# Activation loads two chunks ahead, first gate loads two chunks sooner, and a new spread of single-row work in a two-layer decoder kernel

## The reference, cut to what matters

```
q      = xn @ w_q                          # 8 heads, two halves of 128
v1,i1  = top16(q1 . k1) ; v2,i2 = top16(q2 . k2)
ids, g = top16 of (v1 + v2), softmax       # 16 experts of 16384, per head and token
act    = u[ids] . x                        # 128 experts for each token
w      = g * gelu(act)
y      = sum over experts of w * v[ids]
```

## Time and profile before

| | us |
|---|---|
| median of 3 runs | 3242.73 (3241.24 to 3245.43) |
| the profiled execution, its own time | 3249.34 |
| its span, first to last instruction | 3247.5 |
| TensorE busy in the span | 3202.2 (99%) |
| DVE busy | 2597.5 (80%) |
| ACT busy | 1508.2 (46%) |
| POOL busy | 1191.4 (37%) |
| mean granted TensorE clock | 0.998 |

### The profile page before, as it was taken

The page is one execution under the profiler, slowest core; times in us unless marked ns, Lnnn a source line. Parts: engine busy times, 40 slices in busy tenths (PEclk is TensorE's granted clock), DMA queues, the critical chain, the costliest instruction groups (busy, mean ns, idle before and its releaser), DMA issues.

```text
span 3247.5 us, 54682 instructions
## 1 busy us (share of the span) xinstructions
PE 3202.2 (99%) x19694; PEld 3000.9 (92%) x19694; DVE 2597.5 (80%) x4972; ACT 1508.2 (46%) x2298; POOL 1191.4 (37%) x789
## 2 busy tenths in 40 slices
PE   8999999999999999999999999999999999999998
PEld 7878888999999999999988788889999999999998
DVE  6654449999998889999866544499999888999997
ACT  5553233477773333333345532334777633333333
POOL 1000014335435656555300000143454456665552
PEclk9999999999999999999999999999999999999999
DMA  4214422589999999999821143225999999999996
GB/s 148 78 53 143 142 90 91 194 326 386 400 398 399 357 389 390 413 409 416 310 91 66 53 156 130 97 100 189 346 391 393 405 393 370 390 398 417 415 411 258
DMA packets 232172, 893.29 MB, mean 275 GB/s; under 512 B 23856, under 2 KB 69088, under 8 KB 184128
## 3 DMA queue, kind: packets, MB, share of 16 engines
q1 hardware_dynamic: 112912, 455.25, 37.2%
q0 software_dynamic: 99024, 355.98, 27.8%
q10 hardware_dynamic: 20064, 79.91, 6.2%
HBM read 809.57 MB, written 81.48 MB: 274 GB/s over the span
## 4 chain that ended last, share of the span: by engine, by line
PE 63%; issue 14%; DMA 12%; DVE 8%; POOL 2%; ACT 1%; SPq 0%; DVEq 0%; POOLq 0%; ACTq 0%
PE bank L1506 18%; PE bank L1508 18%; PE bank L1507 18%; DMA act_in<-act_d 9%; PE bank L1815 4%; DVE h L1383 4%; DVE w_lo L1411 2%; POOL lo L568 1%; PE bank L1624 1%; PE bank L1661 1%; DMA rows<-in_u_rows,ids 1%; PE bank L1642 1%; DMA raw<-in_stream 1%; DVE lo L983 1%; ACT hi L626 1%
## 5 line engine op out<-in xcount | busy, mean ns | idle before, releaser
L626 ACT ACTIVATE hi<-raw 128x2048 fp32r<-128x2048 f32 (+2 forms) x338 | 620.6, 1836 | 692.9 <-PE bank L1508 396.1
L1506 PE MATMUL bank<-xT_hi,hi 128*128 128x344 f32 (+1 forms) x2688 | 918.7, 342 | 2.1 <-DVE xT_lo L1033 1.7
L1508 PE MATMUL bank<-xT_hi,lo 128*128 128x344 f32 (+1 forms) x2688 | 905.1, 337 | 0.0
L1507 PE MATMUL bank<-xT_lo,hi 128*128 128x344 f32 (+1 forms) x2688 | 900.3, 335 | 0.0
L983 DVE TENSOR_TENSOR lo<-raw,hi 128x2048 fp32r<-128x2048 f32 (+2 forms) x320 | 698.4, 2183 | 183.1 <-ACT hi L626 180.9
L1506 PE MATMUL bank<-w_hi,hi 128*128 128x344 f32 x2048 | 662.3, 323 | 19.2 <-DVE w_lo L1411 18.6
L1507 PE MATMUL bank<-w_lo,hi 128*128 128x344 f32 x2048 | 655.0, 320 | 0.0
L1508 PE MATMUL bank<-w_hi,lo 128*128 128x344 f32 x2048 | 654.0, 319 | 0.0
L615 POOL DMA_INDIRECT rows<-in_v_rows,ids x256 | 426.1, 1665 | 301.6 <-DVE h L1383 248.2
L1506 PEld LDWEIGHTS bank<-xT_hi,hi 128*128 128x128 f32 x2688 | 504.2, 188 | 32.3 <-issue 5.9
L1508 PEld LDWEIGHTS bank<-xT_hi,lo 128*128 128x128 f32 x2688 | 504.4, 188 | 25.3
(11 more groups left out here) (258 smaller groups left out, 4108.8 us busy)
## 6 DMA issues: line engine op xcount, KB each, us to landing
raw<-in_stream SPq DMA_DIRECT2D x352, 1024.0 KB, 7.6
gate_in<-gate_d SPq DMA_DIRECT2D x96, 384.0 KB, 12.4
act_d<-act_s ACTq DMA_DIRECT2D x92, 352.0 KB, 6.3
gate_d<-gate_s ACTq DMA_DIRECT2D x22, 1472.0 KB, 9.6
act_in<-act_d SPq DMA_DIRECT2D x92, 352.0 KB, 10.0
gate_d<-gate_s ACTq DMA_DIRECT2D x22, 576.0 KB, 13.7
gate_in<-gate_d SPq DMA_DIRECT2D x32, 256.0 KB, 9.6
rows<-in_u_rows,ids POOLq DMA_INDIRECT x256, 10.0
```

The lines of the kernel that those rows point to most:

```text
L626: act.activation(hi[s][:, 0:n], raw[s][:, 0:n], ACT.Copy).then_inc(hi_done, 1)
L1506: pe.matmul(dst, a_[0], b_[0], start=first, stop=False)
L1507: pe.matmul(dst, a_[0], b_[1], start=False, stop=False)
L1508: return pe.matmul(dst, a_[1], b_[0], start=False, stop=last)
```

## The change

It has three parts.

1. The activation of a spilled chunk c is loaded by SP in the place where that of chunk c-2 was loaded before, into one of four buffers, `act_in[0]`, `act_in[1]`, `act_k[0]`, `act_k[1]` by c modulo 4. It waits for `w_lo` of chunk c-4. The four buffers have a semaphore each. ACT's loop over the last stretch runs over four chunks instead of two.
2. The four gate parts of the first slot are issued after the weight loads of q = 48 and 49 instead of 50 and 51.
3. The row operations: 84 instead of 96 by q = 42, and then shares of 41 for an up step, 28 for a kept down step and 24 for a spilled down step. ScalarE's gelu of the rows' dot products and the weighing after it move from q = 70 and 74 to q = 66 and 70.

```diff
-ROWS_IN_G = 96
+ROWS_IN_G = 84
-SHARED = 2
+SHARED, ACT_BUFS = 2, 4
-GATES_AT = {50: (0, 0), 51: (0, 2), 52: (1, 0), 53: (1, 1), 54: (1, 2), 55: (1, 3),
+GATES_AT = {48: (0, 0), 49: (0, 2), 52: (1, 0), 53: (1, 1), 54: (1, 2), 55: (1, 3),
-GATES_FROM, V_FROM = 50, 80
-ROW_GELU_AT, WEIGH_ROWS_AT = 70, 74
-UP_SHARE, DOWN_SHARE, ROWS_END = 16, 13, 2 * C_U - 2
+GATES_FROM, V_FROM = 48, 80
+ROW_GELU_AT, WEIGH_ROWS_AT = 66, 70
+UP_SHARE, KEPT_SHARE, DOWN_SHARE, ROWS_END = 41, 28, 24, 2 * C_U - 2
...
-    shares = [UP_SHARE if x in UP_OF else DOWN_SHARE for x in range(FIND_STEPS + G_STEPS, ROWS_END)]
+    shares = [UP_SHARE if x in UP_OF else KEPT_SHARE if DOWN_OF[x] < KEPT else DOWN_SHARE for x in range(FIND_STEPS + G_STEPS, ROWS_END)]
...
-        act_ld = [sem(f"act_ld{s}") for s in range(2)]
+        act_ld = [sem(f"act_ld{b}") for b in range(ACT_BUFS)]
...
+        def spilled_acts(b):
+            return (act_in, act_k)[b // 2][:, b % 2]
+
+        def acts_loaded(l, c):
+            b = c % ACT_BUFS
+            first = KEPT + (b - KEPT) % ACT_BUFS
+            return act_ld[b], 16 * (l * len(range(first, C_V, ACT_BUFS)) + (c - first) // ACT_BUFS + 1)
...
-                def load_act(j, s):
+                def load_act(v, x):
+                    j, s, b = v * ACT_BUFS // 2 + x // 2, x % 2, x % ACT_BUFS
                     wait_alone(sp, act_out[s], 16 * (l * ACT_PAIRS + j) + 16, sp_passed)
-                    sp.wait_ge(w_done, done + 2 * j + s + 1)
-                    sp.dma_start(act_in[:, s].rearrange("p i t -> p (i t)"), act_d[2 * j + s - KEPT]).then_inc(act_ld[s], 16)
+                    sp.wait_ge(w_done, done + ACT_BUFS * v + x - ACT_BUFS + 1 + CR)
+                    sp.dma_start(spilled_acts(b).rearrange("p i t -> p (i t)"), act_d[ACT_BUFS * v + x - KEPT]).then_inc(act_ld[b], 16)
...
                         load_raw(lp + P_V + v * V_CHUNKS // 2 + c // 2, c % 2)
-                        if not (isinstance(v, int) and v * V_CHUNKS + c < KEPT):
-                            load_act(v * V_CHUNKS // 2 + c // 2, c % 2)
+                        if not last or c + 2 < V_CHUNKS:
+                            load_act(v, c + 2)
...
-                        dve.wait_ge(act_ld[s], 16 * (l * ACT_PAIRS + (c - KEPT) // 2 + 1))
+                        dve.wait_ge(*acts_loaded(l, c))
```

More of the change, by code:

```diff
@@ L472, in acts_of @@
         def acts_of(k, s):
-            return (act_k, act_s, act_in)[k % SPAN // 2][:, s] if isinstance(k, int) and k < KEPT else act_in[:, s]
+            return (act_k, act_s, act_in)[k % SPAN // 2][:, s]
+        def spilled_acts(b):
[4 more added lines that the diff above has]
+            return act_ld[b], 16 * (l * len(range(first, C_V, ACT_BUFS)) + (c - first) // ACT_BUFS + 1)
         @block.sync
@@ L936, in _, with weights_hi @@
                             store_gates(q // PER_SLICE)
-                def weights_hi(c, s):
+                def weights_hi(c, s, b):
                     act.wait_ge(prod_done, l * C_V + c + 1)
@@ L943, in weights_hi @@
                         act.wait_ge(w_used, 2 * (lp + P_V) + c + 1)
-                    act.activation(w_hi[:, s], acts_of(c, s), ACT.Copy).then_inc(w_hi_done, 1)
+                    acts = acts_of(c, s) if isinstance(c, int) and c < KEPT else spilled_acts(b)
+                    act.activation(w_hi[:, s], acts, ACT.Copy).then_inc(w_hi_done, 1)
                 for q in range(FIND_STEPS + G_STEPS, C_V + KEPT):
@@ L952, in _ @@
                     if q + 1 in DOWN_OF:
-                        weights_hi(DOWN_OF[q + 1], (q + 1) % 2)
+                        weights_hi(DOWN_OF[q + 1], (q + 1) % 2, DOWN_OF[q + 1] % ACT_BUFS)
                     if q in UP_OF:
@@ L958, in _, with v_steps @@
                             store_act(UP_OF[q] // 2, q % 2)
[L960 to L968, removed]
+                def v_steps(v, first, end):
+                    for x in range(first, end):
+                        ahead(lp + P_V + v * ACT_BUFS // 2 + x // 2, x % 2)
+                        weights_hi(v * ACT_BUFS + x + 1, (x + 1) % 2, (x + 1) % ACT_BUFS)
+                v_steps(KEPT // ACT_BUFS, KEPT % ACT_BUFS, ACT_BUFS)
+                with act.Fori(KEPT // ACT_BUFS + 1, C_V // ACT_BUFS - 1) as v:
+                    v_steps(v, 0, ACT_BUFS)
+                v_steps(C_V // ACT_BUFS - 1, 0, ACT_BUFS - 1)
                 if l + 1 < DEPTH:
@@ L1400, in weigh_step @@
                     else:
-                        dve.wait_ge(act_ld[s], 16 * (l * ACT_PAIRS + (c - KEPT) // 2 + 1))
+                        dve.wait_ge(*acts_loaded(l, c))
                     dve.wait_ge(gate_ld[v % 2], 16 * GATE_PARTS * (v // 2 + 1))
-                    a_ = acts_of(c, s).rearrange("p i (q t) -> p i q t", t=SLICE)
+                    acts = acts_of(c, s) if c < KEPT else spilled_acts(c % ACT_BUFS)
+                    a_ = acts.rearrange("p i (q t) -> p i q t", t=SLICE)
                     i = 2 * (c % V_CHUNKS)
@@ L1410, in weigh_lo @@
                     dve.wait_ge(w_hi_done, k + 1)
-                    dve.tensor_tensor(w_lo[:, s], acts_of(c, s), w_hi[:, s].bitcast(F32), ALU.subtract).then_inc(w_done, 1)
+                    acts = acts_of(c, s) if c < KEPT else spilled_acts(c % ACT_BUFS)
+                    dve.tensor_tensor(w_lo[:, s], acts, w_hi[:, s].bitcast(F32), ALU.subtract).then_inc(w_done, 1)
                 assert rows_by(ROW_GELU_AT - 1) >= U_ROW_OPS and rows_by(WEIGH_ROWS_AT - 1) <= U_ROW_OPS + E
```

## The result

The changed kernel takes 3276.5 us (3275.2 to 3284.2, 4 runs) against 3244.1 us before (4 runs): ratio 1.0102, 95% interval 1.008 to 1.0124. It is 1% slower: by 32 us between the medians, and by 28.4 us between the spans of the two profiled executions. The forecast was 3238 within 3223 to 3255.

What follows compares the result with a forecast made beforehand. TensorE was taken as busy 3202 of 3247.5 us, so only waits, about 36 us, could be won. The terms -17.4 + 0 + 5 + 8.2 = -4.2 us gave a forecast of 3238, range 3223 to 3255.

Steps and rivals of the forecast that it cites:

- The last stretch: From q 82 on: earlier activation loads and fewer bytes leave 4 us of waits in both layers, -17.4 us.
- The signs named for it: In the profile after: no DVE wait for `act_in` loads in the last stretch, which takes 346 to 349 us.
- Rival E: Last stretch: sooner activation loads only put weight loads later, half of 21 us stays; +2.5 us, 3245; chance 0.10.
- q 43 to 57: Nine more rows and sooner gate parts; 121 us a layer taken, no change; upper end +6.6 us.
- q 58 to 69: Six more rows, all in up steps: 2.5 us a layer, +5 us; ends 0 and +18.
- q 70 to 81: More rows of `v` make DVE too long, 4.1 us a layer: +8.2 us; ends 0 and +13.4.
- A wait in pieces need not cost the clock's 2.7 us: q 43 to 57: short separate waits might avoid the 1.2 GHz loss seen in q 52 to 57, softening the byte limit.
- a credit of 4.4 us for seven row buffers: q 43 to 57 and q 70 to 81: half of the drained buffers, 1.8 MB, counted against the DMA time.
- Rivals C: Up steps slower by DMA bytes, 7.98 us a step against 7.57: +7.6 us, 3250; chance 0.18.
- D: q 58 to 64 slower by POOL, from about 2.0 us for each gather: +9 us, 3251; chance 0.10.
- The gates: q 43 to 57: four gate parts two steps sooner move the same late load two steps forward, to chunk 50.
- DVE's length in q 70 to 77: Four or five `v` rows a step delay DVE: waits of 2.7 us and 1.4 us, together 4.1 us a layer.

Runs made afterwards that it cites:

- part 3 alone: The kernel before with only the new row shares, 84 rows by q = 42, gelu and weighing at q = 66 and 70: ratio 1.0102.
- part 2 alone: The kernel before with only the first four gate parts issued two chunks sooner: ratio 0.9997 (0.9987 to 1.0006).

## Why the prediction was wrong

**The last stretch: right in size, and in its reason.** Forecast -17.4 us, measured -19.5. The reckoning in bytes (3.20 MB a step too much, 3.08 just enough) is borne out from three sides: part 1 gives 3.7 us in one trace and 1.6 in another, near the scatter, part 3 alone 17 (11.3 and 5.6), and half the gather bytes all of it. The signs named for it came too: no wait for `act_in`, and 345.9 and 346.8 us for the stretch (346 to 349 forecast). Rival E's mechanism, loads that come sooner only make others late, is what part 1 does by itself.

**The steps that failed** are the three terms for q 43 to 81, all of them too small and over their upper ends:

| term | taken | upper end | measured |
|---|---|---|---|
| q 43 to 57 | 0 | +6.6 | +14.4 |
| q 58 to 69 | +5 | +18 | +19.6 |
| q 70 to 81 | +8.2 | +13.4 | +15.0 |

(In the second, 1.3 us are the faster up steps of the trace before, which leaves 18.3, at the upper end.)

**First, the clock.** "A wait in pieces need not cost the clock's 2.7 us" was false here. Pieces of 1.8 and 1.9 us cost it as well, 1.6 us each, though three of 1.4 to 1.6 us did not. Slow steps cost 18 us in the changed kernel and 4.2 before; of the difference 2.3, 6.5 and 5.2 us lie in the three terms. These 14 us of the 32.6 between forecast and profile stood in no term; they are over two fifths of the error. Without them the last term would be 9.8, near its 8.2, and the middle one, without the 1.3 as well, 11.8; the first would still be 12.1 where nothing was expected. The prediction had the row (0.94 in q 52 to 57) and counted it as a loss to be won back, but didn't ask whether each new wait would bring one.

**Second, bytes set against the time of too many steps, and buffers as credit.** The bytes of q 43 to 57 were set against all 15 steps, 124.3 us at most. But 38 of the 55 rows are asked for in the first nine: these moved 79.8 x 0.409 = 32.6 MB, 79.2 us at 412 GB/s against the 68.1 that TensorE needs, while the six down steps behind them had room (375 GB/s) and took about as long as before. The nine steps alone took 6.6 and 7.2 us more. Against the bytes stood a credit of 4.4 us for seven row buffers that could be drained; it made 3.3 us a layer into nothing here, and in q 70 to 81 it brought the bytes from 6.7 to 2.3 us, under DVE's 4.1. DVE waited 11.7 us for rows in q 43 to 51 of the first layer alone. How much the buffers really gave wasn't measured by itself.

**Third, two limits at one place.** Rivals C (bytes) and D (POOL) were priced one at a time, each on top of a forecast that took the other as light. The runs show both at work in the up steps: with either one lifted, q 46 to 51 stays 6.5 to 10.6 us over its least, and with both lifted it is at it. Even the upper ends of C and D together, -17.4 + 6.6 + 18 + 13.4 = +20.6, lie 8 us under what was measured. D's condition, about 2.0 us for each gather, was met with gathers halved (1.99) and not in the changed kernel itself (46.0 / 26 = 1.77 in q 58 to 63), where its counterweight is at work: gathers fall to 0.96 us when DVE waits, but by then TensorE is waiting as well.
The Trainium skill (SBUF — State Buffer, "SBUF: two separate sides") gives the lock between DVE and GpSimd, for some kinds of DVE instruction, as one that is held for the whole instruction. The 1.9 to 2.0 us against 0.96 agree with a gather that has to wait out a row operation of DVE; which port it waits at, and whether these row operations are of the kinds named, no run here shows.

**The gates** did what was said: the late load moved two steps forward (TensorE waits for chunk 50 with part 2 alone, for chunk 52 before). In the changed kernel that is mixed with late rows.

**DVE's length in q 70 to 77** was worked out as 4.1 us a layer, and that was about right: with gathers halved, where DVE waits for no row, q 70 to 81 takes 4.7 and 5.1 us over its least, 3.1 and 5.1 without the one slow step, against 4.1. What the term lacked is what comes on top. The changed kernel takes 7.6 and 8.0 us over the least there, 2.7 and 2.4 of them in slow steps, and DVE waits 3.2 us for rows in each layer. TensorE's wait for chunk 76 is 4.3 and 4.9 us in place of the 2 to 3 named as a sign.

**The sum.** -19.5 + 14.4 + 19.6 + 15.0 - 1.1 = +28.4 on the profiled spans. The -1.1, in q 14 to 42, was taken as nothing; as said above, that wait comes and goes between traces.
